# PEER expert sums of the eight sample tokens with samples on partitions; gate products on ScalarE; tile 1 routed earlier

## What is computed

```python
def block(xt):                                    # 128 tokens
    q = (xt @ w_q).reshape(PEER_BLOCK, PEER_HEADS, 2, PEER_DK // 2)
    s = jnp.einsum('thcd,hcnd->thcn', q, keys)
    sv, si = lax.top_k(s, PEER_TOPK)              # 16 best of 128 keys, twice
    ...                                           # 16 best of the 256 sums -> idx, top_s
    g = jax.nn.softmax(top_s, axis=-1)
    a = jnp.einsum('td,thkd->thk', xt, u_tab[idx])
    hk = g * jax.nn.gelu(a, approximate=False)
    return jnp.einsum('thk,thkd->td', hk, v_tab[idx])
h = layer_norm(DN_ALPHA * h + peer_ffn(h, ...), ln_g, ln_b)
```

## Time and profile before

| | before |
|---|---|
| median of 3 runs | 3215.26 us (3214.26 to 3216.42) |
| profiled execution, time and span | 3215.45 us, 3213.5 us |
| TensorE busy (matmul, weight load) | 77%, 65% |
| VectorE, ScalarE, GpSimd busy | 72%, 53%, 38% |
| granted TensorE clock, mean | 0.865 |
| moved by DMA | 1255.97 MB, mean 391 GB/s |
| of it the gathers' queue | 1113.83 MB, 84.7% of the engines' time |

### The profile page before, as it was taken

How to read it: one execution, slowest core, us unless ns; L and a number is a source line. 1 busy time by engine, 2 the same in 40 slices (tenths; PEclk the granted TensorE clock), 3 DMA queues, 4 the chain that set the end, 5 groups by cost and what they waited for, 6 DMA issues and landing times.

```text
span 3213.5 us, 41527 instructions
## 1 busy us (share of the span) xinstructions
PE 2480.3 (77%) x13984; PEld 2082.5 (65%) x13984; DVE 2302.1 (72%) x6345; ACT 1710.0 (53%) x2524; POOL 1218.9 (38%) x1095
## 2 busy tenths in 40 slices
PE   8986889766987878876877787878687665686878
PEld 6655778655676767765766666766576555576665
DVE  2737666886567887778956777677668888678655
ACT  1325456776455754445545685444555555456773
POOL 1113333334433434433433344334344444434441
PEclk9888989977988888997987799999799777678899
DMA  7568999989999999999999899999999999989997
GB/s 294 192 251 359 410 409 383 411 328 390 411 421 420 400 421 421 421 421 396 393 421 421 335 420 414 421 421 421 411 421 421 402 421 418 412 351 421 421 421 288
DMA packets 182531, 1255.97 MB, mean 391 GB/s; under 512 B 21358, under 2 KB 26222, under 8 KB 33584
## 3 DMA queue, kind: packets, MB, share of 16 engines
q0 software_dynamic: 156320, 1113.83, 84.7%
q1 hardware_dynamic: 24416, 136.35, 10.6%
q10 hardware_dynamic: 1584, 3.15, 0.3%
HBM read 1246.78 MB, written 6.50 MB: 390 GB/s over the span
## 4 chain that ended last, share of the span: by engine, by line
DMA 35%; PE 25%; DVE 23%; ACT 7%; DVEq 4%; issue 4%; POOL 1%; SPq 0%; ACTq 0%; POOLq 0%
DMA arena<-in_uv,idx 34%; DVE arena L1655 10%; PE acc L1909 8%; ACT arena L1173 5%; PE bank L1936 5%; PE bank L1927 4%; PE bank L1714 2%; PE acc L1906 2%; DVEq L1561 2%; DMA panel<-in_panels 1%; PE bank L1748 1%; POOL arena L986 1%; ACT L1163 1%; DVE ya L1504 1%; DVE yb L1534 1%
## 5 line engine op out<-in xcount | busy, mean ns | idle before, releaser
L986 POOL DMA_INDIRECT arena<-in_uv,idx x1024 | 1174.0, 1146 | 1758.5 <-PE acc L1909 1522.7
L1909 PE MATMUL acc<-cst,arena 128*128 128x128 f32 x8128 | 1256.7, 317 | 673.0 <-ACT arena L1173 671.3
L1173 ACT ACTIVATE arena<-arena,act_w 128x1024 f32<-128x1024 f32 x1032 | 1129.0, 1141 | 1023.8 <-DVE act_w L1664 1006.9
L1909 PEld LDWEIGHTS acc<-cst,arena 128*128 128x128 f32 x8128 | 1099.4, 164 | 851.8 <-ACT arena L1173 822.1
L1655 DVE CUSTOM_DVE_ANT_0 arena<-arena,h 128x1024 f32<-128x1024 f32 x1024 | 1247.4, 1221 | 450.2 <-DMA arena<-in_uv,idx 431.9
L1936 PE MATMUL bank<-hT,panel 128*128 128x264 f32 (+2 forms) x1856 | 421.7, 382 | 2.3 <-DMA panel<-in_panels 1.3
L1936 PEld LDWEIGHTS bank<-hT,panel 128*128 128x128 f32 x1856 | 344.5, 196 | 51.4 <-issue 2.3
L1163 ACT ACTIVATE act_w<-dots 128x2 f32<-128x2 f32 x520 | 101.6, 195 | 87.8 <-DVE dots L1655 80.5
L1163 ACT ACT_TABLE_LOAD x109 | 139.8, 1283 | 2.0
L1714 PE MATMUL bank<-hT,panel 128*128 128x264 f32 (+1 forms) x512 | 120.4, 394 | 13.5 <-DMA panel<-in_panels 13.5
L1664 DVE TENSOR_TENSOR act_w<-act_w,gate 128x2 f32<-128x2 f32 x512 | 80.5, 157 | 58.0 <-ACT act_w L1163 56.3
(11 more groups left out here) (236 smaller groups left out, 2327.2 us busy)
## 6 DMA issues: line engine op xcount, KB each, us to landing
panel<-in_panels SPq DMA_DIRECT2D x116, 1024.0 KB
arena<-in_uv,idx POOLq DMA_INDIRECT x1024
arena<-in_cache_k POOLq DMA_DIRECT2D x16, 512.0 KB, 6.4
arena<-in_cache_v POOLq DMA_DIRECT2D x16, 512.0 KB, 4.9
arena<-out_y_s POOLq DMA_DIRECT2D x8, 512.0 KB, 9.1
arena<-in_panels SPq DMA_DIRECT2D x4, 1024.0 KB, 8.0
h<-in_h SPq DMA_DIRECT2D x2, 1024.0 KB
out_y_p<-h SPq DMA_DIRECT2D x3, 512.0 KB
```

The source lines that it names most:

```text
L986: nc.gpsimd.indirect_dma_start(uv[:, slot_of(e), :], None, uv_dram[layer], bass.IndirectOffsetOnAxis(ids[:, r:r + 1], 0)).then_inc(gathere ...
L1173: nc.scalar.activation(row, row, ACT.Copy, scale=act_w[:, 1, half, r:r + 1]).then_inc(weighted, 1)
L1909: m = mm(acc[:, c * P:(c + 1) * P], row, const("ident"), is_transpose=True, start=False, stop=True, skip_group_check=True)
```

## The change

Three edits. First, the gate products move from VectorE to ScalarE. Once for each group ScalarE copies eight gates next to its weights (after g_done, a new signal of VectorE, or ixs_ready for the sample), and for each pair, when both dots are there, it makes in a row: the GELU, a drain, two products 128x1 (activation Copy with the GELU as input and the gate as scale), a drain, and both row scalings. VectorE does both dots of a pair in a row, after its background lot. Second, in a sample window ScalarE makes of each weight 8 columns of 128 partitions (s_columns, in the space of s_heads_out) instead of scaling the row, TensorE holds these 8 columns and moves the value row past them in two halves of 512, so the sums stand with tokens on partitions, acc[0:8, :]. ScalarE copies them straight into h, with no "back", and the norm of the sample waits for acc_free. Third, in the first window the last 13 routing pieces of tile 0 end at pair 36 instead of 40, and of tile 1's 33 pieces 25 instead of 17 are dealt out there, over pairs 36 to 64; 8 instead of 16 are left for the first 20 pairs of the window of tile 1.

```diff
 
             lots = [[] for _ in range(8 * HEADS if b < TB else 4)]
             done = place(layer, b) - 1
-            lots[0] += self.back(done // BLOCKS, TILE_ORDER[done // BLOCKS][done % BLOCKS])
+            before = TILE_ORDER[done // BLOCKS][done % BLOCKS]
+            if before < TB:
+                lots[0] += self.back(done // BLOCKS, before)
             for first, last, pieces in lanes:
                 rest, so_far = sum(COST[x.kind] for x in pieces), 0
                 at, base, before = int(2 * first), int(2 * first), None
...
         others = self.others()
         r1, r2 = self.route(0, 1), self.route(0, 2)
         first_window((0, 1, [r[6]]), (1, 2, [r[7]]), (1, 6, n1 + t1 + q[0:2] + r[8:12]), (6, 13, q[2:] + late), (7, 12, r[12:20]),
-                     (12, 20, r[20:]), (20, 32, r1[:17]), (15, 29, others))
+                     (12, 18, r[20:]), (18, 32, r1[:25]), (15, 29, others))
         bg = self.mix(0, 1)
         self.at_panel[bg[0].panel] = "rows"
         bg += self.norm(0, GROUP_TILES[1], False) + self.turn(GROUP_TILES[1], self.ln_of, "norm") + self.features("pq", 0, 1)
         self.last_other_mix = [x for x in bg if x.kind == "mix"][-1]
-        window(0, 1, (0, 10, r1[17:]), (14, 30, bg), (24, 32, r2[:13]))
+        window(0, 1, (0, 10, r1[25:]), (14, 30, bg), (24, 32, r2[:13]))
         lots = steps[1][3] + steps[2][3]
         for j in range(HEADS):
             for b, at in ((2, 36 + 7 * (j // 2) + 3 * (j % 2)), (3, 64 + 2 * j)):
...
                         nc.scalar.activation(r_exs[u % 2], r_tvs[u % 2], ACT.Exp, bias=r_nms[u % 2],
                                              accum_out=r_sums[u % 2]).then_inc(gexp_done, 1)
 
-            def two_gelus(G, q):
+            def two_experts(G, q, b):
 
                 half, s = G % 2, slice(2 * q, 2 * q + 2)
                 act.wait_ge(dot_done, G * GROUP + 2 * q + 2)
-                nc.scalar.activation(act_w[:, 0, half, s], dots[:, half, s], ACT.Gelu).then_inc(gelu_done, 1)
-
-            def two_rows(G, q):
-
-                half = G % 2
-                act.wait_ge(gated, G * 4 + q + 1)
+                nc.scalar.activation(act_w[:, 1, half, s], dots[:, half, s], ACT.Gelu).then_inc(gelu_done, 1)
+                act.drain()
+                for r in range(2 * q, 2 * q + 2):
+                    nc.scalar.activation(act_w[:, 2, half, r:r + 1], act_w[:, 1, half, r:r + 1], ACT.Copy,
+                                         scale=act_w[:, 0, half, r:r + 1])
+                act.drain()
                 for r in range(2 * q, 2 * q + 2):
                     e = G * GROUP + r
+                    if b == TB:
+                        nc.scalar.activation(s_columns[:, r, :], const("group_of")[:, 0:NS], ACT.Copy,
+                                             scale=act_w[:, 2, half, r:r + 1]).then_inc(weighted, 1)
+                        continue
                     if e < FIRST_BY_ROWS:
                         row = uv[:, slot_of(e), D:2 * D]
-                        nc.scalar.activation(row, row, ACT.Copy, scale=act_w[:, 1, half, r:r + 1]).then_inc(weighted, 1)
+                        nc.scalar.activation(row, row, ACT.Copy, scale=act_w[:, 2, half, r:r + 1]).then_inc(weighted, 1)
                         continue
                     if e >= FIRST_BY_ROWS + DIAGS:
                         act.wait_ge(slot_done, e - DIAGS + 1)
                     nc.scalar.activation(diag[:, r % DIAGS, :], const("ident"), ACT.Copy,
-                                         scale=act_w[:, 1, half, r:r + 1]).then_inc(weighted, 1)
+                                         scale=act_w[:, 2, half, r:r + 1]).then_inc(weighted, 1)
                 if G * GROUP + 2 * q == FIRST_BY_ROWS:
                     act.wait_ge(slot_done, FIRST_BY_ROWS)
                     nc.scalar.activation(yb[:], acc[:], ACT.Copy).then_inc(turned_over, 1)
 
+            gates5 = gate[:].rearrange("p b h (a r) -> p b h a r", a=2)
             later = []
             for kind, layer, b, lots in steps:
                 if kind == "alone":
...
                     if len(later) > BEHIND:
                         for x in later.pop(0):
                             background(x)
-                    if t > 0:
-                        two_rows(first_group(layer, b) + (t - 1) // 4, (t - 1) % 4)
-                    two_gelus(G, q)
-                two_rows(G, q)
+                    if q == 0 and b < TB:
+                        act.wait_ge(g_done, place(layer, b) * HEADS + hd + 1)
+                        nc.scalar.activation(act_w[:, 0, G % 2, :], gates5[:, b, hd, t // 4 % 2, :], ACT.Copy)
+                    elif q == 0:
+                        act.wait_ge(ixs_ready, layer + 1)
+                        nc.scalar.activation(act_w[:, 0, G % 2, :], gs8, ACT.Copy)
+                    two_experts(G, q, b)
                 for lot in later:
                     for x in lot:
                         background(x)
...
                 if (layer, b) == (1, TILE_ORDER[1][-1]):
                     continue
                 act.wait_ge(slot_done, (G + 1) * GROUP)
+                if b == TB:
+                    nc.scalar.activation(h[0:NS, TB, :], acc[0:NS, :], ACT.Copy).then_inc(acc_free, 1)
+                    continue
                 done = place(layer, b)
                 if done == 0:
                     for i in range(2):
                         act.wait_ge(k_late[i], 64)
-                else:
+                elif done - 1 in plan.backs:
                     act.wait_ge(bank_full, plan.backs[done - 1][1].n + 1)
                 m = rows(b)
                 nc.scalar.activation(stage[:].rearrange("p (c t) -> p c t", c=C)[:, :, 0:m],
...
                 row = h[0:m, x.b, :]
                 sums = acc[:] if x.first else row
                 if x.tiles is not None and not x.first:
-                    for y in plan.backs[x.tiles]:
-                        read(dve, y)
+                    if x.b == TB:
+                        dve.wait_ge(acc_free, x.tiles + 3)
+                    else:
+                        for y in plan.backs[x.tiles]:
+                            read(dve, y)
                 if x.first:
                     for y in x.part:
                         dve.wait_ge(bank_full, y.n + 1)
...
                 dve.wait_ge(gexp_done, unit + 1)
                 V.reciprocal(r_inv, r_sums[unit % 2])
                 dve.drain()
-                V.tensor_scalar(gate[:, b, hd, :], r_exs[unit % 2], r_inv, None, ALU.mult)
+                V.tensor_scalar(gate[:, b, hd, :], r_exs[unit % 2], r_inv, None, ALU.mult).then_inc(g_done, 1)
 
             def background(x):
 
...
                             for back in (1, 0):
                                 gates(x.b, x.hd - back, x.u - back)
 
-            def dot(e, x_rows):
-
-                G, r = e // GROUP, e % GROUP
-                dve.wait_ge(gathered[slot_of(e)], 16 * (use_of(e) + 1))
-                if r == 0:
-                    dve.wait_ge(gelu_done, G * 4 + 4)
-                V.tensor_tensor_reduce(uv[:, slot_of(e), 0:D], uv[:, slot_of(e), 0:D], x_rows, 1.0, 0.0, ALU.mult, ALU.add,
-                                       dots[:, G % 2, r:r + 1]).then_inc(dot_done, 1)
-
-            def two_weights(layer, b, t):
-
-                G, q = first_group(layer, b) + t // 4, t % 4
-                s = slice(2 * q, 2 * q + 2)
-                dve.wait_ge(gelu_done, SEED_GELU + G * 4 + q + 1)
-                of = gate[:, b, t // 8, t % 8 * 2:t % 8 * 2 + 2] if b < TB else gs8[:, s]
-                V.tensor_tensor(act_w[:, 1, G % 2, s], act_w[:, 0, G % 2, s], of, ALU.mult).then_inc(gated, 1)
+            def two_dots(G, q, x_rows):
+                for r in range(2 * q, 2 * q + 2):
+                    e = G * GROUP + r
+                    dve.wait_ge(gathered[slot_of(e)], 16 * (use_of(e) + 1))
+                    if r == 0:
+                        dve.wait_ge(gelu_done, G * 4 + 4)
+                    V.tensor_tensor_reduce(uv[:, slot_of(e), 0:D], uv[:, slot_of(e), 0:D], x_rows, 1.0, 0.0, ALU.mult, ALU.add,
+                                           dots[:, G % 2, r:r + 1]).then_inc(dot_done, 1)
 
             later = []
             for kind, layer, b, lots in steps:
...
                             background(x)
                     if t == 0:
                         dve.drain()
-                    x_rows = h[:, b, :] if b < TB else x_sample[:]
-                    dot(G * GROUP + 2 * q, x_rows)
-                    if t > 0:
-                        two_weights(layer, b, t - 1)
-                    dot(G * GROUP + 2 * q + 1, x_rows)
-                two_weights(layer, b, t)
+                    two_dots(G, q, h[:, b, :] if b < TB else x_sample[:])
 
 
         @block.tensor
...
             def start_tile(src, m, count):
 
                 pe.wait_ge(acc_free, count + 1)
+                if m == NS:
+                    for half in range(2):
```

(18 more changed lines are left out.)

5 lines of the change are left out of this document (3 added, 2 removed).

## The result

The kernel with the change takes 3189.4 us (3183.1 to 3192.1, 4 runs) against 3214.8 us before: ratio 0.9923 (95% interval 0.9906 to 0.9941). Run again later it took 3191.1 us, ratio 0.9918 (0.9904 to 0.9933). That is 25 to 26 us gained where 58.7 were forecast; the time lies inside the range (3134 to 3192), at its very edge. The profiled execution took 3192.1 us with a span of 3190.1.

What follows compares the result with a forecast made beforehand. The prediction took DMA transfers to bound the kernel: 2983 us at full rate, leaving 230 us of gaps to win. Gains by stretch, less 4 us for ScalarE, summed to 58.7 us, giving 3157 us, range 3134 to 3192.

Steps and rivals of the forecast that it cites:

- The window of tile 1: 640 to 750 us: routing pieces and products leave VectorE, so missing transfer time falls from 23.8 to 3 us, gaining 20.8.
- Rival (a): ScalarE takes VectorE's place as the bound if a pair costs 1.2 us more: 3175 to 3190 us, chance 0.15.
- I cost that at nothing: ScalarE's bank copies stand behind 3.2 us of pair work, but TensorE wants them later: no cost, at most 3 us a lot.
- The reserve: Gather slots come free earlier, a one-time gain for each gap: 3.5 us where background lots are light, 5 where heavy.
- K: Follow-up theory, 1500 to 1570 us: VectorE's work per pair sets the pace; taking work out leaves 3 to 5 us missing.
- The sample: Gaps behind the sample's sum, which gets shorter than its gathers: 13.7 us gained in layer 0, 7.3 in layer 1.
- 460 to 640 us: First window takes the added routing pieces, yet the earlier slot release gains 3 us net (bounds: 11 lost, 8 gained).
- rival (b): The routing only moves its gap: the first window loses what 640 to 750 us wins; about 3175 us, chance 0.12.
- ScalarE's cost of a pair: Products, drains and gates add 0.7 us per pair on ScalarE (bounds 0.4 to 1.2); GELU to first row scaling takes 0.85.
- Rival (d): Slower: ScalarE paces the 109 pairs with a table load ahead of the GELU, costing 76 us: 3233 us, chance 0.05.
- (c): Earlier slot release is worth more, all gaps from 340 to 2870 us go: 3123, more likely near 3137 us; chance 0.12.
- (e): Freed slots' gathers wait for something else, such as GpSimd's issue, and gaps stay: within 0.2% of before, chance 0.04.

Runs made afterwards that it cites:

- experiment 2: Kernel before with one part of the change alone, three kernels; the one cited here routes tile 1 sooner: 3206.9 us, ratio 0.9973.
- The doubled products: Changed kernel with each pair's two 128x1 gate products and their drain made a second time on ScalarE: 3204.2 us, ratio 0.9958.
- sample_routes: Kernel before with the sample's new sum and the sooner routing, gate products still on VectorE: 3196.0 us, ratio 0.9928.
- wide_no_gates: Changed kernel with the routing of tile 1's last two heads over 36 pairs instead of 20, gate products back on VectorE: 3189.8 us, ratio 0.9927.

## Why the prediction was right and where it was wrong

**The window of tile 1, 20.8 forecast, 9.3 measured: the step that failed.** The working took VectorE's 24 us out of 110, set the new length by the transfers' 86 us, and left 3: each microsecond taken from VectorE was to shorten the stretch by one. That fails in two ways. First, without any product on ScalarE: the routing alone takes the same 20.4 us out and wins 10, with VectorE at 88.75 and ScalarE at 92.68 of 110 us (experiment 2). VectorE was nearly full before, but its busy time was not all that set the length; what else did was not isolated. Second, the working never redid the sum for ScalarE. That sum was there to be made: 83.57 us in the window, and 0.7 us for each of the 17 or 18 pairs that the profiles of before have in it, are 96 us; the routing that leaves takes only some 2.3 of them along, by the rows of the window before (two exponentials, their sums and a table load). That is more than the 89 us to which the stretch was meant to shrink. The kernel after gets 19 or 20 pairs through in the 110 us, with ScalarE at 106.04. Of the 22.5 us that are new there, the products and the gates are 10.1, table loads 6.4 (21 instead of 16). I charged ScalarE's full stretches once, 4 us, at 1850 to 1900 us (none was lost there), and called it idle on average otherwise. Rival (a) had this second half in kind, with 0.15, and the time at the upper end of its 3175 to 3190; but its condition, 1.2 us a pair, was not met, the pair costs what was forecast.

**"I cost that at nothing": wrong at one place.** The prediction saw that ScalarE's copies out of the banks would stand behind 3.2 us of pair work, and said TensorE wants them later. At the turn of the tile it wants them at once: 4.21 us of waiting, 10.50 for GpSimd, 4 to 5 us of missing transfers more than before at 640 to 660 us. "Up to 3 us for that lot" was the right kind of number, for one pair's work; it was two pairs' work. How much of the 4 to 5 us is this wait isn't shown: the second profile of after waits 2.6 us there and misses 7.0, and the routing alone, with no product on ScalarE, misses 3.8.

**The reserve, 3.5 to 5 us for each gap.** Slots do come free earlier, by as much as worked out. Timelines of before (second profile) and after (second profile) at the same heavy lots:

```profile
1514.74 0.08 DVE L1655 DVE_READ_ACCUMULATOR2_ANT dots<- 128x1 f32 x1
...
1521.88 2.19 ACT L1173 ACTIVATE arena<-arena,act_w 128x1024 f32<-128x1024 f32 x2 [0.85 <-DVE act_w L1664]
```

```profile
1508.94 0.08 DVE L1672 DVE_READ_ACCUMULATOR2_ANT dots<- 128x1 f32 x1
...
1509.06 0.20 ACT L1166 ACTIVATE act_w<-dots 128x2 f32<-128x2 f32 x1 [0.22 <-DVE dots L1672]
1509.34 0.48 ACT L1169 ACTIVATE act_w<-act_w 128x1 f32<-128x1 f32 x2
1509.89 2.19 ACT L1180 ACTIVATE arena<-arena,act_w 128x1024 f32<-128x1024 f32 x2
```

From the second dot's end to the row scalings 7.06 us before, 0.87 after. What a reserve is worth is another number: how much longer a gather's request stands ahead of its landing. The page's median us from issue to landing, second profile of before and after:

```profile
arena<-in_uv,idx POOLq DMA_INDIRECT x1024, 17.6
```

```profile
arena<-in_uv,idx POOLq DMA_INDIRECT x1024, 19.9
```

It is 2.3 us, about one gather, not two. My reading is that the lag is long only inside the heavy stretch, when the reserve is already being spent, and that the step "5 where they are heavy" took the lag of the burst for the reserve before it; the median is over all gathers, so this is argued, not shown. At 1500 to 1570 us even of 2.3 us only 1.2 came out (8.3 and 8.6 against 9.5 and 9.8, and 6.3 to 10.6 in all other kernels). And most of that is not the release: the sample alone and the routing alone, with the old order, miss 8.5 and 8.8. Why the earlier release wins next to nothing there isn't settled; K was hardly put to the test.

**The sample.** Layer 1 was right within 1.4 us, its own stall of 11 us included. In layer 0 the tile starts as soon behind the last dot as forecast (5.9 us for 6.2). The 7.4 us left instead of 3 are VectorE's: it is busy 71.65 of 80 us in 1770 to 1850, and only 3.4 and 3.7 us are missing in the two kernels that hand tile 0's routing out more thinly. The prediction wrote that VectorE "gets its 9.76 us back" for that load, and didn't add that the load then meets the full rate of gathers.

**Right.** 1050 to 1070 us (3.5 against 3.4). 460 to 640 us (3.4 against 3), where the added routing pieces cost nothing; rival (b) is out. ScalarE's cost of a pair: 0.20 + 0.48 + drains, 0.83 us from GELU to scaling against 0.85; the product takes 286 ns against 0.30 from the earlier trace rows. Rival (d): 111 table loads stand in front of GELUs in after, 109 in before, and outside 640 to 750 us no stretch lost by more than the two profiles of a kernel differ. So the loads' cost stayed hidden, but for the one window where ScalarE was full. Rivals (c) and (e) are out.

**The rule against this change.** The Trainium skill (ScalarE: Activation LUTs, Rules for kernel authors) sends multiplies to VectorE. The doubled products put a price on it here: 0.56 us of ScalarE's time a pair costs 13 us in all, 8.6 missing in the one window, and none from 1900 to 2870 us. Another 3.4 came behind the sample. By the rule the products should go back; they are in sample_routes, 0.05 to 0.10% slower, and in wide_no_gates, equal by the intervals. So the trace agrees with the rule in the window of tile 1, where ScalarE is full (8.6 us missing against 12.5, once VectorE is relieved), and shows nothing for it elsewhere.

## What to carry to other kernels

When work leaves an engine that bounds a stretch, redo the sum of every other engine over the same stretch at the new, shorter length, with what the change gives to it: here 83.57 + 12 against 89. And don't take the relief of a full engine for the gain one for one: 20.4 us less of VectorE's work alone won 10. A product's row in the profile is not what its engine gets back either, where instructions overlap: 0.16 us each, and 0.08 came back. Before background work is moved into "idle" engines, look at TensorE as well as at the two that one is relieving.

## What the runs showed of the hardware

Two 128x1 activations with a scale from memory take 0.48 us together behind a drain, and the drain leaves 0.07 to 0.09 us between two instructions. With 8 stationary columns a product of 128x512 in f32 is issued every 0.43 us at a granted clock of 1.00 (in after from 1747 us on, loads of 0.09 us with 0.34 between them) and about every 0.86 at 0.57 (1743 to 1747 us). An expert's value row is four of them, 1.7 us at 1.00, which a gather every 2.5 us hides. With a 128x128 stationary block and 8 moving columns TensorE was busy 28.00 of 28 us and was granted 0.50. A lead of the same code ended between 210.3 and 219.3 us in 19 profiles; the later ones go with a lower clock at 110 to 120 us, and the rest has no cause on record. That range is more than most of the effects above, which is why they are read by stretch and not by span.
